# Joining the output and state-space stages, and one-pass spreading of the attention weights

## The reference, cut to what matters

```
# first layer, attention: groups g are weighed by a softmax over their log-sums, per position s and head h
wts = jax.nn.softmax(jnp.stack(lses, axis=0), axis=0)
o_attn = jnp.einsum('gbsh,gbshe->bshe', wts.astype(x.dtype), jnp.stack(outs, axis=0))
...
# first layer, end
out = merged @ w_out + b_out
res = DEEPNORM_ALPHA * x.astype(jnp.float32) + (gate * out).astype(jnp.float32)
return (_layer_norm(res) * ln_g + ln_b).astype(x.dtype)
...
# second layer, start
x = layer_norm(x, ln_emb_g, ln_emb_b)
z = x @ w_in[i]
xs, gs, cq, ckv, kr, gm = jnp.split(z, IN_SPLIT_POINTS, axis=-1)
ys = s5_branch(xs, a_re[i], a_im[i], log_dt[i], b_re[i], b_im[i], c_re[i], c_im[i],
               d_skip[i], w_glu[i], b_glu[i]) * jax.nn.silu(gs)
ym = mla_branch(cq, ckv, kr, cos, sin, ...) * jax.nn.silu(gm)
...
# s5_branch: a diagonal complex recurrence over positions, 32 groups of 64 states and 16 channels
dt = jnp.exp(log_dt.astype(f32))[:, None]
mag = jnp.exp(dt * a_re)
ab_re = mag * jnp.cos(dt * a_im)
ab_im = mag * jnp.sin(dt * a_im)
h[l] = ab * h[l-1] + k * (b @ u[l]);  y[l] = Re(c @ h[l]) + d_skip * u[l];  y = gelu(y)
```

## Time and profile before

| what | value |
|---|---|
| median of 3 runs | 2340.42 us (2340.11 to 2340.95) |
| the profiled execution | 2337.36 us |
| its span in the profile | 2335.5 us |
| PE busy | 2141.1 us, 92% |
| DVE, ACT, POOL busy | 1065.5, 639.0, 265.1 us |
| mean granted clock of PE | 0.961 |
| attention stage | about 624 to 1416 us |
| output projection | 1418 to 1568 us |
| state-space stage | 1568 to 1766 us |

### The profile page before, as it was taken

The page is one execution under the profiler, slowest core; times in us unless marked ns, Lnnn a source line. Parts: engine busy times, 40 slices in busy tenths (PEclk is TensorE's granted clock), DMA queues, the critical chain, the costliest instruction groups (busy, mean ns, idle before and its releaser), DMA issues. The chain is left out here.

```text
span 2335.5 us, 23211 instructions
## 1 busy us (share of the span) xinstructions
PE 2141.1 (92%) x9435; PEld 1548.0 (66%) x9435; DVE 1065.5 (46%) x1729; ACT 639.0 (27%) x1046; POOL 265.1 (11%) x137
## 2 busy tenths in 40 slices
PE   4896999999899999999999999859798989989997
PEld 1453547588777777777777886636556754559875
DVE  5686879870122322322312235779543323452255
ACT  4522212122223233332333210111214434230232
POOL 0110001012211111111111121100001100000000
PEclk9997999999999999999999999979898999999999
DMA  7311122201201111110112114013101120012100
GB/s 252 122 63 45 32 90 90 59 20 54 99 28 37 36 46 36 38 37 28 37 37 99 49 37 158 27 26 141 21 0 47 41 108 1 1 60 86 54 36 36
DMA packets 126107, 135.24 MB, mean 58 GB/s; under 512 B 14487, under 2 KB 106074, under 8 KB 124833
## 3 DMA queue, kind: packets, MB, share of 16 engines
q1 hardware_dynamic: 120707, 111.57, 14.9%
q0 software_dynamic: 5152, 22.15, 2.5%
q10 hardware_dynamic: 142, 0.03, 0.0%
HBM read 116.77 MB, written 15.80 MB: 57 GB/s over the span
## 5 line engine op out<-in xcount | busy, mean ns | idle before, releaser
L171 PE MATMUL banks<-h_hi,fr_w_rest 128*128 128x512 f32 x1152 | 468.7, 407 | 10.5 <-DVE h_rest L906 5.4
L172 PE MATMUL banks<-h_rest,fr_w_hi 128*128 128x512 f32 x1152 | 453.0, 393 | 0.0
L173 PE MATMUL banks<-h_hi,fr_w_hi 128*128 128x512 f32 x1152 | 452.9, 393 | 0.0
L171 PEld LDWEIGHTS banks<-h_hi,fr_w_rest 128*128 128x128 f32 x1152 | 218.7, 190 | 88.2 <-issue 37.6
L173 PEld LDWEIGHTS banks<-h_hi,fr_w_hi 128*128 128x128 f32 x1152 | 218.3, 189 | 47.6
L172 PEld LDWEIGHTS banks<-h_rest,fr_w_hi 128*128 128x128 f32 x1152 | 219.0, 190 | 42.5 <-issue 1.0
L1486 DVE COPY arena<-banks 128x768 f32<-128x768 f32 (+1 forms) x64 | 52.8, 825 | 371.9 <-PE banks L1249 371.9
L1172 POOL TENSOR_TENSOR fr_w_rest<-arena,fr_w_hi 128x1024 fp32r<-128x1024 f32 x45 | 107.6, 2390 | 554.2 <-ACT fr_w_hi L1334 554.2
L489 PE MATMUL banks<-arena 128*128 128x512 f32 x256 | 125.2, 647 | 35.5 <-issue 28.4
L1357 ACT ACTIVATE arena<-banks,arena 128x512 f32<-128x512 f32 x92 | 63.2, 687 | 277.6 <-PE banks L173 277.5
L765 DVE SCALAR_TENSOR_TENSOR arena<-arena 128x1024 f32<-128x1024 f32 (+5 forms) x108 | 131.0, 1213 | 3.7
(11 more groups left out here) (345 smaller groups left out, 3451.4 us busy)
## 6 DMA issues: line engine op xcount, KB each, us to landing
arena<-in_w_in SPq DMA_DIRECT2D x80, 512.0 KB, 3.8
arena<-in_w_ada POOLq DMA_DIRECT2D x6, 2048.0 KB, 18.5
arena<-in_x SPq DMA_DIRECT2D x4, 1024.0 KB, 18.9
arena<-in_fwd SPq DMA_DIRECT2D x16, 256.0 KB, 4.8
filter_spectra<-arena POOLq DMA_DIRECT2D x2, 2048.0 KB, 6.6
arena<-in_inv SPq DMA_DIRECT2D x16, 256.0 KB, 2.6
arena<-filter_spectra SPq DMA_DIRECT2D x2, 2048.0 KB, 8.4
arena<-in_w_out SPq DMA_DIRECT2D x8, 512.0 KB, 8.1
```

What stands on the lines that cost most here:

```text
L171: nc.tensor.matmul(out, ll, rh, start=start, stop=False)
L172: nc.tensor.matmul(out, lh, rl, start=False, stop=False)
L173: return nc.tensor.matmul(out, lh, rh, start=False, stop=stop)
```

## The change

**Spreading.** `wts` gets 36 columns: columns 32 to 35 repeat columns 0 to 3, the rest is zero. The transposes give 36 rows. ACT copies all of them rounded to the one-pass type, DVE overwrites rows 32 to 35 with the rest (value minus rounded value), and `sel` holds its 0/1 rows twice. Four one-pass matmuls of 36 rows replace four fp32 matmuls of 4.

**Norm.** Three passes (scale and shift by the statistics, times gamma, plus beta) become two.

**One stage.** `first_output` and `s5_states` become `output_and_states` with no meeting between them. SP issues the loads of the state stage among those of x; x2's rows are stored one by one instead of in one transfer. DVE does the poles ahead of row 0, the powers in row 1 and the input factors in row 3, each behind the pass that frees PSUM. PE does input tiles 0 and 1 between its last two sets of row transposes.

**Order inside it.** Four latent tiles stand ahead of the transposes of the state inputs, four behind the state inputs' matmuls. DVE waits for the Toeplitz copies behind the first quarter's products instead of ahead of them.

```diff
@@ dilated_attention
-    wts = K.at(o, 8, 4); o += 32
+    wts = K.at(o, 8, 36); o += 288
...
+            sp.wait_ge(cleared, 1)
+            for r in (0, 32):
+                sp.dma_start(sel_raw[r:r + 4, :, :], io["pick"]...).then_inc(sel_in, 16)
...
+            pool.wait_ge(K.yhy_out, 16)
+            nc.gpsimd.memset(wts[:, :, :], 0.0)
+            nc.gpsimd.memset(sel_raw[0:36, :, :], 0.0).then_inc(cleared, 1)
...
-                        last = nc.tensor.matmul(PS[:, 2 * g + h, :], sel[0:4, g, :], wrow[0:4, h * 512:(h + 1) * 512], start=True, stop=True)
+                        last = nc.tensor.matmul(PS[:, 2 * g + h, :], sel[0:36, g, :], wrow[0:36, h * 512:(h + 1) * 512], start=True, stop=True)
...
-                nc.scalar.copy(wrow[0:4, :], flat(PS[0:4, 4:6, :])).then_inc(wrow_ready, 1)
+                if j == 0:
+                    act.wait_ge(sel_in, 32)
+                    nc.scalar.copy(sel[0:36, :, :], sel_raw[0:36, :, :]).then_inc(sel_ready, 1)
+                    act.wait_ge(sel_ready, 1)
+                nc.scalar.copy(wrow[0:36, :], flat(PS[0:36, 4:6, :])).then_inc(wrow_hi, 1)
...
+                link(nc.vector.tensor_copy(wts[:, :, 32:36], wts[:, :, 0:4]), weighed)
                 if more:
                     dve.wait_ge(pv_done, UNITS * (j + 1))
                     take_value_rows(j + 1, 0)
                     take_value_rows(j + 1, 1)
+                dve.wait_ge(wrow_hi, j + 1)
+                nc.vector.tensor_tensor(wrow[32:36, :], flat(PS[32:36, 4:6, :]), wrow[32:36, :].bitcast(fp32), ALU.subtract).then_inc(wrow_ready, 1)
@@ RowNorm
-        self.link(nc.vector.tensor_scalar(row, row, st[:, 12:13], st[:, 15:16], ALU.subtract, ALU.mult))
-        self.link(nc.vector.tensor_tensor(row, row, gamma, ALU.mult))
-        self.link(nc.vector.tensor_tensor(row, row, beta, ALU.add), *([final] if final else []))
+        self.link(nc.vector.scalar_tensor_tensor(row, row, st[:, 12:13], gamma, ALU.subtract, ALU.mult))
+        self.link(nc.vector.scalar_tensor_tensor(row, row, st[:, 15:16], beta, ALU.mult, ALU.add), *([final] if final else []))
@@ output_and_states, SP
+            def spill(r):
+                sp.wait_ge(row_ready, r + 1)
+                sp.dma_start(K.x2_rows[:, r * D:(r + 1) * D], x2r[:, r, :]).then_inc(rows_out, 16)
+            sp.dma_start(ldt, bcast_rows(io["log_dt_2"][0])).then_inc(dt_in, 16)
+            load_class(0)
+            load_class(1)
...
+            for r in range(4, NT):
+                load_class(r)
+                spill(r - 4)
+            for r in range(4, NT):
+                spill(r)
+            sp.wait_ge(rows_out, 16 * NT)
+            sp.wait_ge(tr, 2 * NT)
+            sp.dma_start(wlat, ...).then_inc(lat_in, 16)
@@ output_and_states, PE
+            def inputs(t):
...
+                pe.wait_ge(tr_taken, 2 * t + 2)
+                if t < 4:
+                    pe.wait_ge(t_read, 7 if t < 2 else 8)
...
+            inputs(0)
+            inputs(1)
+            to_columns(NT - 1)
+            pe.wait_ge(c_in, 64)
+            pe.wait_ge(tr_taken, 2 * NT)
...
+            for t in range(2, TC):
+                inputs(t)
...
             pe.wait_ge(xs_ready, TC)
+            pe.wait_ge(lat_in, 16)
+            latents(0, 4)
+            pe.wait_ge(lat_ready, 4)
             pe.wait_ge(c_ready, 1)
...
-            pe.wait_ge(lat_in, 16)
             pe.wait_ge(v_read, 1)
-            for i in range(NT):
...
+            latents(4, NT)
@@ output_and_states, DVE
+            poles()
+            dve.wait_ge(K.vec_in, 80)
+            for r in range(NT):
+                dve.wait_ge(mm, r + 1)
...
+                link(nc.vector.tensor_tensor(work[:, r % 2, :], src, vec[:, 0, :], ALU.add), read)
+                if r == 1:
+                    powers()
+                if r == 3:
+                    input_factors()
+                dve.wait_ge(gated, r + 1)
...
-            dve.wait_ge(toeplitz, 16 * TC)
             for q in range(4):
...
                 tt(tmp[:, 2, :, :], tmp[:, 2, :, :], tmp[:, 3, :, :], ALU.subtract)
+                if q == 0:
+                    dve.wait_ge(toeplitz, 16 * TC)
```

More of the change, by code:

```diff
@@ L1609, in first_output @@
+    args = K.at(o, 4, 16); o += 64
+    trig = K.at(o, 4, 16); o += 64
+    assert o <= X2T
+    are, aim = cols2[:, 0:16], cols2[:, 16:32]
+    wlat, lat, squares, ss = K.at(LATW, KT, 448), K.at(LAT, NT, 448), K.at(LATS + 16, 384), K.at(LATS, NT, 2)
+    K.x2_rows = nc.dram_tensor("x2_rows", (P, NT * D), fp32, kind="Internal").ap()
+    over_c = lambda a: a.unsqueeze(2).to_broadcast([P, 16, 16])
     with ExitStack() as ctx:
[L1610 removed]
+        s = lambda n: K.sem("os_" + n)
@@ L1674, in _ @@
-        @block.vector
-        def _(dve):
-            chain = Count(order)
-            def link(ins, signal=chain):
-                signal.by(ins)
-                dve.wait_ge(signal.sem, signal.n)
-            norm = RowNorm(nc, dve, link, stat, Count(var), std)
-            rows, used, read = Count(row_ready), Count(x_used), Count(t_read)
-            dve.wait_ge(K.vec_in, 80)
-            for r in range(NT):
-                dve.wait_ge(mm, r + 1)
-                src = PS[:, 2 * (r % 2):2 * (r % 2) + 2, :].rearrange("p a b -> p (a b)")
-                link(nc.vector.tensor_tensor(work[:, r % 2, :], src, vec[:, 0, :], ALU.add), read)
-                dve.wait_ge(gated, r + 1)
-                dve.wait_ge(x_in[r % 2], 16 * (r // 2 + 1))
-                row = x2r[:, r, :]
-                link(nc.vector.scalar_tensor_tensor(row, xin[:, r % 2, :], ALPHA, work[:, r % 2, :], ALU.mult, ALU.add), used)
-                norm(row, vec[:, 1, :], vec[:, 2, :])
-                norm(row, vec[:, 3, :], vec[:, 4, :], rows)
@@ new lines, in input_factors @@
+            def input_factors():
+                link(nc.vector.tensor_scalar(v["nr"], v["abre"], 1.0, None, ALU.subtract))
+                tt(v["ta"], v["nr"], are, ALU.mult)
+                tt(v["tb"], v["abim"], aim, ALU.mult)
+                tt(v["kre"], v["ta"], v["tb"], ALU.add)
+                tt(v["kre"], v["kre"], v["den"], ALU.mult)
+                tt(v["ta"], v["abim"], are, ALU.mult)
+                tt(v["tb"], v["nr"], aim, ALU.mult)
+                tt(v["kim"], v["ta"], v["tb"], ALU.subtract)
+                tt(v["kim"], v["kim"], v["den"], ALU.mult)
+                dve.wait_ge(b_in, 32)
+                complex_product(kB[:, 0, :, :], kB[:, 1, :, :], braw[:, 0, :, :], braw[:, 1, :, :], over_c(v["kre"]), over_c(v["kim"]), small)
+                for ri in range(2):
+                    for t in range(TC):
+                        chain.by(nc.vector.tensor_copy(rev[:, ri, t, :], pw[:, ri, TC - 1 - t, :]))
+                dve.wait_ge(order, chain.n)
@@ new lines, in _ @@
+            norm = RowNorm(nc, dve, link, stat, Count(var), std)
+            rows, used, read = Count(row_ready), Count(x_used), Count(t_read)
+            poles()
+            dve.wait_ge(K.vec_in, 80)
+            for r in range(NT):
+                dve.wait_ge(mm, r + 1)
+                src = PS[:, 2 * (r % 2):2 * (r % 2) + 2, :].rearrange("p a b -> p (a b)")
+                link(nc.vector.tensor_tensor(work[:, r % 2, :], src, vec[:, 0, :], ALU.add), read)
[4 more added lines that the diff above has]
+                dve.wait_ge(gated, r + 1)
+                dve.wait_ge(x_in[r % 2], 16 * (r // 2 + 1))
+                row = x2r[:, r, :]
+                link(nc.vector.scalar_tensor_tensor(row, xin[:, r % 2, :], ALPHA, work[:, r % 2, :], ALU.mult, ALU.add), used)
+                norm(row, vec[:, 1, :], vec[:, 2, :])
+                norm(row, vec[:, 3, :], vec[:, 4, :], rows)
@@ L1964, in _ @@
                     link(last, Count(c_ready))
+                else:
+                    chain.by(last)
+            dve.wait_ge(order, chain.n)
             for j0 in (0, 8):
```

316 lines of the change are left out of this document (142 added, 174 removed).

## The result

The changed kernel takes 2320.9 us (median of 4 executions, 2318.9 to 2322.3) against 2340.7 for the kernel before on the same chip: ratio 0.9914 [0.9897, 0.9931]. Forecast were 2290.0 us, 2280 to 2304. The sign was right; of 50.5 us, 20 came.

What follows compares the result with a forecast made beforehand. PE's holes were taken to bound the output projection (DVE-bound rows) and state stage; attention was PE-bound. Savings 10.8 + 6.8 + 32.0 + 0.85 = 50.5 us gave 2286.9 profiled, 2290.0 median; range 2280 to 2304.

Steps and rivals of the forecast that it cites:

- the last of the state part: State outputs: after its hole PE starts cold, costing 3.0 us; output matmuls begin 35.0 us earlier, net 32.0 for the block.
- the rival: State outputs: once started cold, the output matmuls stay on 1.2 GHz; 2321 us, or 2305 if half their spacing does not stretch; chance 0.06.
- stand where DVE would have waited 2.52 for POOL, so they add 2.73 and 3.53: Row loop, rows 1 and 3: powers (5.25 us) and input factors (6.05) partly hidden by DVE's 2.52 us wait for POOL.
- the fused norm pass: Row loop: the norm's scale pass of 0.81 us goes, two norms a row; a row takes 14.82 us instead of 16.52.
- The spreading: Attention: four one-pass matmuls take 0.93 us a set instead of 3.63; 2.70 saved, 10.8 us in four sets.
- the dips: Attention: PE's low clock behind each of four spreading sets goes, 6.8 us; rival that they stay, 2297 us, chance 0.15.
- The first load landed late: Before row 0: the state constants' first input, a 16 KB broadcast issued at 1418, lands at 1426.1.
- the first row's pass: Start of the row loop: DVE's constants end at 1434.3, 2.0 us after the first matmuls end at 1432.31.
- From the end of the last row to the state transposes: Joined stage: last row ends at 1560.0, state transposes start at 1631.1, after six input tiles and four latent tiles.
- from these to the first output: State part: transposes start at 1631.1; outputs wait until DVE has all four quarters' products read at 1695.2.
- the wait in front of it: Before the state outputs: PE's 11.2 us stall ahead of the latents becomes 14 us behind them, on DVE's chain.

## Why the prediction was wrong

**The step that failed** is the last of the state part: "After its hole PE starts cold: the latents after 11.18 us of waiting took 51.20 - 8 x 6.01 = 3.1 us more, the first input tile 2.9. I take 3.0." The hole was forecast, with its place, its length and what ends it. Its price was carried over from matmuls of 448 and 512 columns to ones of 128, and in the outputs those never brought the clock back: 26.1 us for 3.0, which is 23.1 of the 32. With the hole filled the outputs took 26.2 us less. I had this as a rival, at 2321 with a chance of 0.06, and the time came out at 2320.9. The mechanism was that one; the agreement in the time is luck. The rival's price was 31 us more than the forecast, for outputs that take twice their time; they took 1.77 times it, and the 8 us between happen to be what the second error below and a longer stretch behind the outputs cost, less what the first stage gained. (The distance that the prediction gives as 33.8 us is 33.9 by its own two rows, and ends at the start of the last addition.) Against the rival I had put that the outputs ran 34 us at full clock after a hole of 1.25 us. That shows that they hold a clock they have, and not that they can raise it; and by the runs above they do not even hold it reliably: 1.24 us of waiting lost it in 7 of 8 executions without the split. The row that spoke for the rival, a transpose of 1.97 us for 1.09, has the same shape and stands behind the same kind of hole. It shows that 128-column matmuls start cold too, and not for how long they stay so; but no row at all spoke for 3.0 us.

Whether the columns keep the clock down is argued, not shown. Two of three output instructions also fill only 64 of the 128 rows (L1822 and L1823), and few filled rows lowered the clock in the attention; no run has the outputs with other columns or other rows.

**The second step that failed** is "stand where DVE would have waited 2.52 for POOL, so they add 2.73 and 3.53". They added 4.85 and 5.58. A small DVE operation with two operands in the on-chip memory did not run beside POOL's product, it waited for it: 2.05 us lost in each of the two rows. What follows from longer rows was left out as well: PE's holes grow to 5 and 6 us, its clock falls, and DVE waits 4.2 us for it. Moving the constants gave back 14.6 us in the loop: 4.85 + 5.58 + 4.2. The Trainium skill (SBUF — State Buffer, "SBUF: two separate sides", and GPSIMD Engine Reference, "Key points") says that VectorE and GpSimd share a pair of ports as an exclusive lock, also when a vector operation has two inputs there. The trace agrees, with 2.43 us for 0.38, and the rule would have brought the sum nearer by 4 us.

**A small size off:** the fused norm pass takes 1.28 us, not 1.23, four a row: a row is 15.07 and not 14.82 us, 2.0 over eight rows.

**What held.** The spreading: 1.12 us from set to next matmul with 0.93 forecast, clock 1.0 behind the sets, attention 17.7 us shorter with 17.6 forecast, and the reason for the dips, the narrow matmuls, is shown by the fp32 set over 128 rows. The first load landed late, 7.5 us behind its issue with 8.0 forecast, and the first row's pass began 15.9 us behind PE's first matmul with 16.2 forecast. Part of that is luck: it was PE's matmuls that ended last there, by 0.2 us, because they ran into a dip (29.53 us for 27.83) that no term had. From the end of the last row to the state transposes 71.5 us with 71.1 forecast; from these to the first output 64.3 with 64.1; the wait in front of it 14.6 with 14, ended by DVE.

**What no step had:** the first stage, whose code is untouched, is 5.7 us shorter. It is no chance of one execution: the first attention copy lies at 624.5 and 625.7 in the two profiles whose attention is that of the kernel before, and at 619.2 to 621.8 in all twelve with a changed one. It does not come through whole: the kernel with only the spreading changed lost 5.8 us behind the outputs again. Where it happens can be read, DVE first in the kernel before, then in the changed one:

```profile
411.68 2.25 DVE L837 TENSOR_TENSOR arena<-arena 128x2 f32<-128x2 f32 x1
```

```profile
410.52 0.16 DVE L837 TENSOR_TENSOR arena<-arena 128x2 f32<-128x2 f32 x1
```

POOL's product starts at 411.51 in the one and at 410.84 in the other. The tiny operation comes 0.2 us behind it there, and 0.3 ahead of it here, and 2.1 us hang on that. So it is in all fourteen profiles: behind POOL's start, by 0.10 and 0.17 us, it took 2.32 and 2.25 us, and ahead of it, by 0.06 to 0.97, it took 0.16. Eleven microseconds on it happens once more (eight passes in 9.94 us for 7.91), PE waits 4.5 us for DVE, and comes out of that on 1.2 GHz until 434. Why the phase of the two engines follows the attention's form was not tried; it stays open.

**Still open** is also why the same hole of 1.24 us costs the clock in 7 of 8 executions without the split, in 1 of 4 with the split and without the wait for the reads, and in 1 of 46 in the order of the kernel before. The matmuls on both sides of it are the same in the first and the last. A dependence on the phase would fit; no run tells it.

## What to carry to other kernels

Price a cold start by the matmuls that run behind the hole, not by the hole: behind 11.18 us of waiting the 448-column ones lost 3.1 us (on half clock for under 6), while 190 instructions of 128 columns ran 59 us at half of it. Where small matmuls follow a wait, close the wait, with work moved there or with a few matmuls that compute nothing (four here, 27 us). A wait for POOL was no free place for DVE work with two operands in the on-chip memory; look for a slot where DVE waits for PE or a load.

## What the runs showed of the hardware

- Output matmuls of 128 columns in fp32, a third of them over 128 rows and the others over 64, kept a full clock for 33 us when no hole stood in front of them, kept it in most executions of one order behind a hole of 1.24 us, lost it 1 to 2.2 us behind the same hole in others, and did not regain it in 48 to 59 us of unbroken work.
- Matmuls of 448 columns behind 11.18 us of waiting had it back in under 6 us (0.50, 0.50 and 0.56 in the three stretches of 2 us from 1677.7 in the kernel before, then 1.00).
- Fp32 matmuls that fill 4 rows of 128 for 3.6 us lowered the clock behind them (0.51 to 0.66 behind the four sets); over 128 rows, of the same duration, they did not (1.00).
- A DVE product of two 128x16 or even 128x2 tiles takes 0.16 to 0.2 us alone and over 2 us behind the start of POOL's 2.36 us product. Which of the two starts first decides, by as little as 0.1 us.
- A pass over 128x1024 with a per-partition scalar and a tensor (scalar_tensor_tensor) takes 1.28 us in the norm and 1.23 with a constant as scalar.
